# Half of the 64x64 matmuls of the mixers' solve move to the two crossed quadrants of TensorE; GpSimd copies a transposed inverse for them

## The chip, the cores and the metric

The kernel runs on one core of one Trainium2 chip. The metric is the time of one execution on the device, in microseconds (us). The kernel before takes 1534.42 us (median of 3 runs, 1533.93 to 1536.74).

## What is computed

Two small transformer blocks, one after the other, on 256 tokens of width 1024. The change touches only the first block, whose two layers each begin with a mixer; these are called m0 and m1 in the kernel. A mixer has a gated delta rule (in both directions, 4 heads of 128) and an HGRN2 scan beside it. The delta rule needs, for each head, chunk of 64 tokens and direction, the inverse of a unit triangular 64x64 matrix:

```
a = jnp.where(strict, jnp.einsum('bhntd,bhnsd->bhnts', kb, k) * decay, 0.0)
t_inv = lax.linalg.triangular_solve(a + eye, jnp.broadcast_to(eye, a.shape),
                                    left_side=True, lower=True, unit_diagonal=True)
u = jnp.einsum('bhnts,bhnsv->bhntv', t_inv, v * beta[..., None])
w = jnp.einsum('bhnts,bhnsd->bhntd', t_inv, kb * jnp.exp(gc)[..., None])
```

With 4 heads, 4 chunks and 2 directions that is 32 such matrices in a layer. Everything else (projections, convolutions, feed-forward parts, the second block's attention) stays as it is.

## The kernel before

Five engines run their own instruction lists, written out by hand in the order in which they run: TensorE (PE), ScalarE (ACT), VectorE (DVE), GpSimd (POOL) and SyncE for the DMAs. Semaphores join them. An engine that waits for one holds back all that stands behind the wait in its own list. Weights arrive in chunks of 128x2048; ACT rounds a chunk to the high half WH, DVE subtracts to get the low half WL, and PE multiplies with both. Eight PSUM banks are handed out in turn.

The inverses of one direction d (0 or 1) are 16 units of 64x64, eight in the upper 64 partitions and eight in the lower 64, in the buffer XIv; XTv holds their transposes. The solve doubles the inverted blocks level by level (lv 1 to 6). A level is:

- `dn_y(d, lv)` on PE: 16 matmuls of 64x64, those of the upper 64 partitions in one quadrant of the PE array and those of the lower 64 in the opposite one. It waits until the level before has been placed in XIv.
- `dn_y` on ACT: copies the 128x512 product from PSUM to YBv.
- `dn_z(d, lv, 0)` on PE: 16 matmuls of the transposed inverse XTv with YBv. It waits for that copy and for the transposed inverse of the level before.
- `placed(d, lv)` on DVE: a predicated copy of 128x512 from PSUM into XIv under the mask of the level.
- `back(d, lv)` on DVE: transposes XIv into XTv by 32x32 blocks.

The first level is made by `dn_first` on DVE from the matrices themselves. At level 5 PE computes both sides (`dn_z(d, 5, 0)` and `dn_z(d, 5, 1)`) and ACT copies the 32-wide corners of both (`dn_z5`). Level 6 joins the two halves (`dn_y6`, `dn_z6`), and already runs in the two crossed quadrants. `blocks_out` on ACT copies XTv into the full 128x128 form.

Between the steps of the solve stands the work of the HGRN2 part: `z_in(n)` (two subtractions of 128x512 on DVE), `hg_exp(n)` (an exponential of 128x1024 on ACT), `hg_mul(g)` (a product of 128x1024 on DVE), `hg(g)` on PE, and `kept(g)` (a predicated copy on DVE). It goes from DVE to ACT to PE and back: `hg(7)` on PE, the last of them, needs `hg_exp(14)` of ACT, and that needs `z_in(14)` of DVE. PE has pieces of projections between (`zproj`, `gate`), and DVE and ACT prepare the weight chunks (`chunk`).

Of the kernel before, what the change touches and what calls it, by code (L numbers as in the profile page):

```python
# [133 lines left out]
def program(nc, a):  # L134
    P_AT, P_W = par_layout()
    ctx = ExitStack()
    with ctx:
# [151 lines left out]
        HALF = (slice(0, 64), slice(64, 128))  # L289
        att = SB[:, 11264:13312]  # L290
# [42 lines left out]
        def level_mask(kind, lv):  # L333
            return MKv[:, kind, lv, 0:64].unsqueeze(1).to_broadcast([128, 8, 64])
# [80 lines left out]
        def tensor(e):  # L415
# [149 lines left out]
            def mixer(l):  # L565
# [83 lines left out]
                def side_placed(d, lv, side):  # L649
                    w.wait_ge(*(A if lv == 5 else V)["placed", st, d, lv, side])  # L650

                def dn_y(d, lv):
                    w.wait_ge(*V["pair", st, 3, d])
                    side_placed(d, lv - 1, 0)
                    p = bank(st, "y", d, lv)
                    for m in range(8):
                        for h in HALF:
                            last = mm(p[h, m * 64:m * 64 + 64], at_d(d, 1 - m // 4)[h, m % 4, h], XIv[h, d, m], True, True)
                    last.then_inc(*P.up("ps", st, "y", d, lv))
                    ps.give(st, "y", d, lv)  # L660

                def dn_z(d, lv, side):
                    w.wait_ge(*A["y", st, d, lv])
                    side_placed(d, lv - 1, 1)
                    p = bank(st, "z", d, lv, side)
                    for m in range(8):
                        for h in HALF:
                            x, y = XTv[h, d, m], YBv[d][h, m]
                            last = mm(p[h, m * 64:m * 64 + 64], *((x, y) if side == 0 else (y, x)), True, True)
                    last.then_inc(*P.up("ps", st, "z", d, lv, side))  # L670
                    ps.give(st, "z", d, lv, side)

                def dn_y6():
# [3 lines left out]
                    for m in range(8):  # L677
                        for d in range(2):
                            last = mm(p[HALF[1 - d], m * 64:m * 64 + 64], at_d(d, 1 - m // 4)[HALF[d], m % 4, HALF[1 - d]],
                                      XIv[HALF[d], d, m], True, True)  # L680
# [3 lines left out]
                def dn_z6():  # L684
# [4 lines left out]
                    for m in range(8):  # L689
                        for d in range(2):  # L690
                            last = mm(p[HALF[d], m * 64:m * 64 + 64], YBv[0][HALF[1 - d], m], XTv[HALF[1 - d], d, m], True, True)
# [3 lines left out]
                def hg(g):  # L695
# [20 lines left out]
                    ps.give(st, "hg", g, 1)  # L716
# [96 lines left out]
                dn_z(1, 1, 0)  # L813
                dn_z(0, 1, 0)
# [3 lines left out]
                dn_z(1, 2, 0)  # L818
                hg(0)
                dn_y(1, 3)  # L820
                dn_z(0, 2, 0)
                dn_z(1, 3, 0)
# [3 lines left out]
                dn_z(0, 3, 0)  # L826
                dn_z(1, 4, 0)
                dn_y(0, 4)
                hg(1)
                dn_z(0, 4, 0)  # L830
                dn_y(1, 5)
                hg(2)
                dn_z(1, 5, 0)
                dn_z(1, 5, 1)
# [394 lines left out]
        def scalar(e):  # L1229
# [57 lines left out]
            def mixer(l):  # L1287
# [145 lines left out]
                def dn_z5(d, side):  # L1433
                    kind = d if side == 0 else 1 - d
                    w.wait_ge(*P["ps", st, "z", d, 5, side])
                    for b in range(2):
                        cp(corner((XIv, XTv)[side][:, d], b, kind), corner(units(ps[st, "z", d, 5, side][:, :]), b, kind),
                           "placed", st, d, 5, side, of=ps.out(st, "z", d, 5, side))

                def blocks_out(d):  # L1440
                    waits(A["placed", st, d, 5, 1], P["ps", st, "row", 3, 1] if d else P["ps", st, "y6"])
                    for b in range(2):
                        cp(XTF[d][HALF[b], :, HALF[b]], XTv[HALF[b], d], "blocks out", st, d)
# [117 lines left out]
                dn_z5(1, 1)  # L1561
                dn_y(0, 5)
                hg_exp(9)
                hg_exp(8)
                blocks_out(1)
                dn_z5(1, 0)
                dn_z5(0, 0)
# [3 lines left out]
                dn_z5(0, 1)  # L1571
# [407 lines left out]
        def vector(e):  # L1979
# [126 lines left out]
            def mixer(l):  # L2106
# [158 lines left out]
                def dn_first(d):  # L2265
                    waits(A["ident", st], V["pair", st, 3, d])
                    for b in range(2):
                        cpred(XTv[HALF[b], d].rearrange("p (j h) n -> p j h n", j=2),
                              block_mask(b, 1 - d, 0, 4).unsqueeze(1).to_broadcast([64, 2, 4, 64]),
                              AT6[HALF[b], 3 - 2 * d:5 - 2 * d, :, HALF[b]], "placed", st, d, 0, 1)  # L2270
# [124 lines left out]
                z_in(6)  # L2395
                kept(2, after=1)
# [9 lines left out]
                z_in(13)  # L2406
                z_in(12)
# [559 lines left out]
        def gpsimd(e):  # L2967
# [5 lines left out]

            for st in ("m0", "m1"):
                for d in (1, 0):
                    w.wait_ge(*(P["ps", st, "row", 3, 1] if d else P["ps", st, "y6"]))
                    zeros(XTF[d][HALF[1 - d], :, HALF[d]], "zeros", st)
# [159 lines left out]
```

## Time and profile before

| | us |
|---|---|
| median of 3 runs | 1534.42 |
| the profiled execution, its span | 1535.2 |
| PE busy in it | 1508.5 |
| DVE busy | 1200.7 |
| ACT busy | 1015.8 |
| POOL busy | 8.3 |
| solve of m0, from its first matmul on PE to hg(7) | 123.8 to 176.8 |
| solve of m1, from its first matmul on PE | 577.2 |

The profile holds one execution; its span is 0.8 us above the median of the runs. Of an engine it gives when each instruction started and how long it took. Times in it count from the start of the span. A matmul in fp32 shows as two records (two passes), so a step of 16 matmuls is 32 records. A busy PE is not PE at its peak: a pass shows its whole latency, and passes overlap.

### The profile page before, as it was taken

The page shows a single profiled execution, that of the slowest core. Times are in us where ns is not written, and L with a number is a line of the kernel's source. Part 1 is how long each engine was busy: PE and PEld are TensorE (multiplying, and loading weights), DVE is VectorE, ACT ScalarE, POOL GpSimd, SP SyncE. Part 2 cuts the span into 40 slices and gives each one's busy share as a digit, 9 for nine tenths or more (in the row PEclk, how much of TensorE's full clock was granted, in tenths as well). Part 3 has the DMA queues.
Part 4 walks back from the last instruction along what each step waited for, and adds up shares of the span by engine and source line. Part 5 has one row for each costly group of instructions (what it writes and reads, how often), then busy time and mean ns, then how long its engine had stood idle before and what let it go on. Part 6 is the DMA issues. An engine that isn't in the chain of part 4 may idle for free.

```text
span 1535.2 us, 29830 instructions
## 1 busy us (share of the span) xinstructions
PE 1508.5 (98%) x12702; PEld 1403.2 (91%) x12702; DVE 1200.7 (78%) x1693; ACT 1015.8 (66%) x1566; POOL 8.3 (1%) x18
## 2 busy tenths in 40 slices
PE   8999999999999999999999999999999998999998
PEld 8899999988889999999988889968999897899997
DVE  7999766889758799667898768875888578688864
ACT  7786865667646776765776546685777457677753
POOL 0000000000000000000000000000000001000000
PEclk9999999999999999999999999999999999999999
DMA  7522135555554422244655546402655543255551
GB/s 290 192 89 107 56 138 193 200 187 193 207 177 158 158 98 85 84 166 165 236 193 182 212 165 249 155 2 85 218 193 187 193 144 135 83 202 187 190 192 55
DMA packets 35700, 245.55 MB, mean 160 GB/s; under 512 B 4208, under 2 KB 4592, under 8 KB 6512
## 3 DMA queue, kind: packets, MB, share of 16 engines
q1 hardware_dynamic: 35568, 243.65, 44.3%
q8 instruction: 100, 1.64, 0.4%
q14 instruction: 32, 0.26, 0.0%
HBM read 242.58 MB, written 1.05 MB: 159 GB/s over the span
## 4 chain that ended last, share of the span: by engine, by line
PE 84%; DVE 10%; ACT 4%; DMA 1%; issue 1%; SPq 0%; DVEq 0%; ACTq 0%
PE PS L420 83%; DVE WL L1984 2%; DVE SB L1993 1%; DVE SB L1984 1%; DVE SA L1984 1%; ACT WH L1237 1%; ACT SB L1234 1%; DMA RAW<-w_in 1%; PE PS L423 1%; ACT SB L1911 1%; DVE SB L2259 1%; DVE SA L1993 0%; DVE SA L2161 0%; DMA X<-xt 0%; DVE SM L1984 0%
## 5 line engine op out<-in xcount | busy, mean ns | idle before, releaser
L420 PE MATMUL PS<-XHL,WH 128*128 128x256 f32 (+2 forms) x4080 | 846.8, 300 | 6.2 <-DVE WL L1984 3.5
L420 PEld LDWEIGHTS PS<-XHL,WH 128*128 128x128 f32 (+1 forms) x4080 | 644.8, 187 | 43.1 <-issue 5.6
L420 PE MATMUL PS<-XHL,WL 128*128 128x256 f32 (+1 forms) x2392 | 669.5, 280 | 0.0
L1237 ACT CAST WH<-RAW 128x2048 fp32r<-128x2048 f32 (+1 forms) x235 | 427.4, 1822 | 270.8 <-PE PS L420 259.0
L1984 DVE TENSOR_TENSOR WL<-RAW,WH 128x2048 fp32r<-128x2048 f32 (+1 forms) x235 | 511.9, 2181 | 113.2 <-ACT WH L1237 109.4
L420 PEld LDWEIGHTS PS<-XHL,WL 128*128 128x128 f32 (+1 forms) x2392 | 448.3, 187 | 0.4
L420 PE MATMUL PS<-INHL,WH 128*128 128x512 f32 (+1 forms) x1216 | 334.2, 344 | 0.0
L420 PE MATMUL PS<-INHL,WL 128*128 128x256 f32 x960 | 270.0, 281 | 0.0
L420 PEld LDWEIGHTS PS<-INHL,WH 128*128 128x128 f32 x1216 | 210.0, 188 | 27.6
L420 PEld LDWEIGHTS PS<-INHL,WL 128*128 128x128 f32 x960 | 181.2, 189 | 0.0
L1984 DVE TENSOR_TENSOR SB<-SB 128x512 f32<-128x512 f32 (+2 forms) x162 | 108.8, 674 | 14.5 <-ACT SB L1234 11.4
L1237 ACT COPY SB<-PS 128x256 f32<-128x256 f32 (+4 forms) x198 | 84.6, 462 | 42.7 <-PE PS L420 31.5
L1993 DVE SCALAR_TENSOR_TENSOR SB<-SB,PR 128x254 f32<-128x254 f32 (+2 forms) x212 | 95.6, 491 | 15.0 <-ACT SB L1234 11.4
L1234 ACT ACTIVATE SB<-SB,PR 128x256 f32<-128x256 f32 x132 | 78.6, 596 | 17.4 <-DVE SB L1984 17.4
L1234 ACT ACTIVATE SB<-SB 128x512 f32<-128x512 f32 (+3 forms) x103 | 66.0, 643 | 12.4 <-DVE SB L1984 11.1
L420 PE MATMUL PS<-SB 64*64 64x64 f32 (+2 forms) x1680 | 73.1, 227 | 0.6 <-DVE SB L2263 0.6
L420 PEld LDWEIGHTS PS<-SB 64*64 64x64 f32 (+1 forms) x1680 | 66.4, 140 | 3.9 <-DVE SB L2263 0.9
L420 PE MATMUL PS<-SA 128*64 128x64 f32 (+6 forms) x784 | 67.9, 288 | 0.6 <-DVE SA L1984 0.6
L1984 DVE TENSOR_TENSOR SB<-PS,SM 128x512 f32<-128x512 f32 (+2 forms) x65 | 43.9, 677 | 27.6 <-PE PS L420 22.3
L1275 ACT ACTIVATE XHL<-X,PR 128x256 fp32r<-128x256 f32 x56 | 25.1, 501 | 48.3 <-DVE X L1984 23.8
L420 PEld LDWEIGHTS PS<-SA 128*64 128x64 f32 (+3 forms) x784 | 47.2, 157 | 8.7 <-issue 4.1
L1984 DVE TENSOR_TENSOR X<-X,PS 128x256 f32<-128x256 f32 (+1 forms) x72 | 31.7, 449 | 30.0 <-PE PS L420 28.9
(156 smaller groups left out, 1446.0 us busy)
## 6 DMA issues: line engine op xcount, KB each, us to landing
RAW<-w_in SPq DMA_DIRECT2D x51, 1024.0 KB, 4.8
RAW<-w_up SPq DMA_DIRECT2D x44, 1024.0 KB, 4.8
RAW<-f_in SPq DMA_DIRECT2D x44, 1024.0 KB, 4.7
RAW<-w_down SPq DMA_DIRECT2D x22, 1024.0 KB, 4.8
RAW<-f_out SPq DMA_DIRECT2D x22, 1024.0 KB, 4.7
RAW<-a_w_in SPq DMA_DIRECT2D x10, 1024.0 KB, 5.0
RAW<-w_out SPq DMA_DIRECT2D x8, 1024.0 KB, 4.8
RAW<-w_bdn SPq DMA_DIRECT2D x4, 1024.0 KB, 4.8
```

The lines of the kernel that those rows point to most:

```text
L420: return e.matmul(out, l, r, start=start, stop=stop, skip_group_check=True)
L423: return e.transpose(out, x, ident[0:k, 0:k])
L1234: e.activation(out, x, f, bias=bias, scale=scale).then_inc(*A.up(*key, of=of))
L1237: e.copy(out, x).then_inc(*A.up(*key, of=of))
L1275: e.mul(halves_of(st)[0][:, s], X[:, s], norm_gain(st, k)).then_inc(*A.up("x hi", st, k))
L1911: e.activation(pb[:, r * 384 + lo:r * 384 + hi], ps[st, "sc", t_, r][:, lo:hi], ACT.Exp, bias=s[:, i:i + 1], accum_out=s[:, 4 + i:5 + i]). ...
L1984: e.tensor_tensor(out, x, y, op).then_inc(*V.up(*key, of=of))
L1993: e.scalar_tensor_tensor(out=out, in0=x, scalar=s, in1=y, op0=op0, op1=op1).then_inc(*V.up(*key, of=of))
L2259: e.copy_predicated(out, m, data).then_inc(*V.up(*key, of=of))
```

## The change

In every step of levels 1 to 5 half of the units go through the crossed quadrants, so that four quadrants have work. For that the lower half's units are stored turned by four places (`place`). Products whose rows come from the upper partitions go to one PSUM bank and those from the lower to another, so that `dn_y` and `dn_z` take two banks each, and what evacuates them works on two halves of 256 columns. `dn_z` needs XTv of four units in the other 64 partitions: GpSimd copies them (`shifted`, two copies of 64x256 for a direction and level) into the new buffer XTS after `back`. The second side of level 5 is no longer a matmul step: `back5` on DVE transposes the new corners of XIv into XTv, after ACT has copied them (`dn_z5`). The schedules of the engines change where steps fall away or are added; `hg` banks are given back one step later.

```diff
+        XTS = SB[:, 7680:8192].rearrange("p (d m n) -> p d m n", d=2, m=4)
+        YH = [y.rearrange("p (r m n) -> p r m n", r=2, m=4) for y in YBs]
...
+        def place(b, m):
+
+            return (m + 4 * b) % 8
...
                 def dn_y(d, lv):
                     w.wait_ge(*V["pair", st, 3, d])
                     side_placed(d, lv - 1, 0)
-                    p = bank(st, "y", d, lv)
-                    for m in range(8):
-                        for h in HALF:
-                            last = mm(p[h, m * 64:m * 64 + 64], at_d(d, 1 - m // 4)[h, m % 4, h], XIv[h, d, m], True, True)
+                    p = row_banks("y", d, lv)
+                    for m in range(4):
+                        o = slice(m * 64, m * 64 + 64)
+                        for f in range(2):
+                            for b in range(2):
+                                last = mm(p[b][HALF[b ^ f], o], at_d(d, 1 - f)[HALF[b], m, HALF[b]],
+                                          XIv[HALF[b], d, place(b, m + 4 * f)], True, True)
...
-                def dn_z(d, lv, side):
+                def dn_z(d, lv):
                     w.wait_ge(*A["y", st, d, lv])
                     side_placed(d, lv - 1, 1)
-                    p = bank(st, "z", d, lv, side)
...
+                    w.wait_ge(*G["shifted", st, d, lv - 1])
+                    p = row_banks("z", d, lv)
+                    for m in range(4):
+                        o = slice(m * 64, m * 64 + 64)
+                        for f in range(2):
+                            for b in range(2):
+                                r = b ^ f
+                                x = XTS[HALF[r], d, m] if f else XTv[HALF[b], d, place(b, m)]
+                                last = mm(p[r][HALF[b], o], x, YH[d][HALF[r], b, m], True, True)
...
                 hg(2)
-                dn_z(1, 5, 0)
-                dn_z(1, 5, 1)
+                dn_z(1, 5)
                 dn_y(0, 5)
                 zproj(2, 1)
                 hg(3)
-                dn_z(0, 5, 0)
+                dn_z(0, 5)
                 hg(4)
                 dn_y6()
-                dn_z(0, 5, 1)
                 zproj(3, 0)
...
                 def dn_y(d, lv):
                     waits(P["ps", st, "y", d, lv], V["k sum", st, 3] if d == 0 else V["bb", st])
-                    cp(YBv[d], units(ps[st, "y", d, lv][:, :]), "y", st, d, lv, of=ps.out(st, "y", d, lv))
+                    for r in range(2):
+                        cp(YBs[d][:, r * 256:r * 256 + 256], ps[st, "y", d, lv, r][:, 0:256], "y", st, d, lv,
+                           of=ps.out(st, "y", d, lv, r))
...
+                def dn_z5(d):
+                    w.wait_ge(*P["ps", st, "z", d, 5])
+                    for r in range(2):
+                        z = ps[st, "z", d, 5, r][:, 0:256].rearrange("p (m n) -> p m n", m=4)
+                        for b in range(2):
+                            cp(corner(XIv[:, d, 4 * r:4 * r + 4], b, d), corner(z, b, d), "placed", st, d, 5, 0, of=ps.out(st, "z", d, 5, r))
...
                 def placed(d, lv):
-                    w.wait_ge(*P["ps", st, "z", d, lv, 0])
-                    cpred(XIv[:, d], level_mask(d, lv), units(ps[st, "z", d, lv, 0][:, :]), "placed", st, d, lv, 0, of=ps.out(st, "z", d, lv, 0))
+                    w.wait_ge(*P["ps", st, "z", d, lv])
+                    for r in range(2):
+                        z = ps[st, "z", d, lv, r][:, 0:256].rearrange("p (m n) -> p m n", m=4)
+                        cpred(XIv[:, d, 4 * r:4 * r + 4], level_mask(d, lv, 4), z, "placed", st, d, lv, 0, of=ps.out(st, "z", d, lv, r))
+
+                def back5(d):
+                    w.wait_ge(*A["placed", st, d, 5, 0])
+                    for b in range(2):
+                        blocks_turned(corner(XTv[:, d], b, 1 - d), corner(XIv[:, d], b, d), "placed", st, d, 5, 1)
...
+            def shifted(st, d, lv):
+
+                w.wait_ge(*V["k out", st, 3])
+                w.wait_ge(*V["placed", st, d, lv, 1])
+                for b in range(2):
+                    e.tensor_copy(XTS[HALF[1 - b], d], XTv[HALF[b], d, place(b, 4):place(b, 4) + 4]).then_inc(*G.up("shifted", st, d, lv))
...
+                for lv in range(5):
+                    for d in (1, 0):
+                        shifted(st, d, lv)
```

Two places show how the lists move. The first is DVE in m0 after `placed(0, 4)`. SA holds the HGRN2 operands, MK the masks, PS is PSUM. Before, `z_in(6)` (two subtractions) is followed at once by `kept(2)`, `z_in(9)`, `hg_mul(3)`, `z_in(8)` and `hg_mul(4)`:

```order
L1984 TENSOR_TENSOR SA<-SA 128x128x4 x2
L2259 COPY_PREDICATED SB<-MK,PS 128x512 [waits s_dve_done,s_pe_group_done]
L1984 TENSOR_TENSOR SA<-SA 128x64x8 x2
L1984 TENSOR_TENSOR SA<-SA 128x1024 [waits s_act_done]
L1984 TENSOR_TENSOR SA<-SA 128x64x8 x2
L1984 TENSOR_TENSOR SA<-SA 128x1024 [waits s_act_done]
L2263 STREAM_TRANSPOSE SB<-SB 128x512 [waits s_dve_done]
```

And after the change, from the same `z_in(6)` on:

```order
L2007 TENSOR_TENSOR SA<-SA 128x128x4 x2
L2286 STREAM_TRANSPOSE SB<-SB 32x8x32 [waits s_act_done]
L2286 STREAM_TRANSPOSE SB<-SB 32x8x32
L2282 COPY_PREDICATED SB<-MK,PS 128x512 [waits s_dve_done,s_pe_group_done]
L2007 TENSOR_TENSOR SA<-SA 128x64x8 x2
L2007 TENSOR_TENSOR SA<-SA 128x1024
L2007 TENSOR_TENSOR SA<-SA 128x64x8 x2
```

The two transposes of `back5(1)` stand between, and the first of them waits for ACT.

The second place is ACT at the same time. Before: the copies of four `dn_y` steps, `hg_exp(7)` and `hg_exp(6)` (x2), the two corner copies of `dn_z5(1, 1)`, the copy of `dn_y(0, 5)`, `hg_exp(9)` and `hg_exp(8)`:

```order
L1237 COPY SB<-PS 128x512 [waits s_pe_group_done] x4
L1234 ACTIVATE SA<-SA 128x1024 [waits s_dve_done] x2
L1237 COPY SB<-PS 32x8x32 [waits s_pe_group_done]
L1237 COPY SB<-PS 32x8x32
L1237 COPY SB<-PS 128x512 [waits s_pe_group_done]
L1234 ACTIVATE SA<-SA 128x1024 [waits s_dve_done] x2
```

After, from the last `dn_y` copy ahead of the exponentials on:

```order
L1259 COPY SB<-PS 128x256 [waits s_pe_group_done]
L1259 COPY SB<-PS 128x256
L1256 ACTIVATE SA<-SA 128x1024 [waits s_dve_done] x2
L1259 COPY SB<-PS 32x4x32 [waits s_pe_group_done]
L1259 COPY SB<-PS 32x4x32 x3
L1259 COPY SB<-PS 128x256 [waits s_pe_group_done]
L1259 COPY SB<-PS 128x256
L1256 ACTIVATE SA<-SA 128x1024 [waits s_dve_done] x2
```

The corner copies, now of XIv and four of them, still stand behind `hg_exp(6)`, which waits for `z_in(6)` of DVE.

## Rows read from the trace of the kernel before

**Rows 1.** The page: the span, and each engine's busy time.

```profile
span 1535.2 us, 29830 instructions
PE 1508.5 (98%) x12702; PEld 1403.2 (91%) x12702; DVE 1200.7 (78%) x1693; ACT 1015.8 (66%) x1566; POOL 8.3 (1%) x18
```

**Rows 2.** Windows of m0: length; busy us of PE, PEld, DVE, ACT, POOL; clock; DMA.

```profile
114.00:134.60 20.60, 19.77 (x353) 19.14 (x353) 20.47 (x30) 14.48 (x30) 0.00 (x0) 1.00 0.31 114
134.60:156.50 21.90, 21.90 (x536) 21.20 (x537) 20.80 (x30) 12.18 (x17) 0.00 (x0) 1.00 0.27 98
156.50:175.00 18.50, 18.43 (x340) 17.57 (x339) 18.40 (x26) 16.73 (x22) 0.52 (x1) 1.00 0.10 31
182.00:200.00 18.00, 18.00 (x132) 16.91 (x131) 5.97 (x4) 10.63 (x13) 0.00 (x0) 1.00 0.23 71
```

**Rows 3.** The chain that ended last, 108 to 182 us: start, us, what.

```profile
133.39 1.15 DVE SA L1984
...
134.58 37.37 PE PS L420 x846
```

**Rows 4.** Timeline of PE: start, us, instructions [idle before, releaser].

```profile
142.50 5.00 PE L420 MATMUL PS<-SB 64*64 64x64 f32 x160
...
148.51 2.08 PE L420 MATMUL PS<-SB 64*64 64x64 f32 x64
...
160.81 1.91 PE L420 MATMUL PS<-SB 64*64 64x64 f32 x64
...
176.77 1.15 PE L420 MATMUL PS<-SA 128*64 128x64 f32 x32
```

**Rows 5.** Timeline of DVE in m0.

```profile
118.64 0.87 DVE L1993 SCALAR_TENSOR_TENSOR SA<-SA,SM,SB 128x256 f32<-128x256 f32 x2
145.56 0.73 DVE L2259 COPY_PREDICATED SB<-MK,PS 128x512 f32<-128x512 uint8 x1 [0.62 <-PE PS L420]
148.63 1.29 DVE L1984 TENSOR_TENSOR SA<-SA 128x512 f32<-128x512 f32 x2 [0.23 <-PE PS L420]
151.07 1.28 DVE L1984 TENSOR_TENSOR SA<-SA 128x512 f32<-128x512 f32 x2
173.71 1.29 DVE L1984 TENSOR_TENSOR SA<-SA 128x512 f32<-128x512 f32 x2
```

**Rows 6.** DVE groups by shape, 114 to 177 us: busy us, mean ns.

```profile
L1984 DVE TENSOR_TENSOR SA<-SA 128x512 f32<-128x512 f32 x28 | 17.7, 682 | 0.4 <-PE PS L420 0.4
L1984 DVE TENSOR_TENSOR WL<-RAW,WH 128x2048 fp32r<-128x2048 f32 x5 | 11.4, 2272 | 0.0
L1984 DVE TENSOR_TENSOR SA<-SA 128x1024 f32<-128x1024 f32 x8 | 9.7, 1219 | 0.0
```

**Rows 7.** Timeline of ACT in m0.

```profile
152.38 1.06 ACT L1234 ACTIVATE SA<-SA 128x1024 f32<-128x1024 f32 x1 [0.20 <-DVE SA L1984]
153.74 0.75 ACT L1237 COPY SB<-PS 32x256 f32<-32x256 f32 x2 [0.29 <-PE PS L420]
...
175.04 1.06 ACT L1234 ACTIVATE SA<-SA 128x1024 f32<-128x1024 f32 x1 [0.61 <-DVE SA L1984]
```

**Rows 8.** A GpSimd group by shape, whole span: busy us, mean ns.

```profile
L2986 POOL COPY SA<-SB 32x512 f32<-32x512 f32 x4 | 2.8, 694 | 349.9 <-DVE SB L1984 349.7
```

**Rows 9.** Timelines of GpSimd and DVE around 1280 us.

```profile
1280.11 2.95 POOL L2986 COPY SA<-SB 32x512 f32<-32x512 f32 x4 [349.75 <-DVE SB L1984]
...
1281.86 0.72 DVE L1984 TENSOR_TENSOR SM<-SM 128x4 f32<-128x4 f32 x2
1282.50 2.71 DVE L1984 TENSOR_TENSOR WL<-RAW,WH 128x2048 fp32r<-128x2048 f32 x1
```

**Rows 10.** Windows around a fall of PE's clock; columns as in rows 2.

```profile
1291.00:1295.70 4.70, 1.76 (x14) 1.06 (x14) 4.04 (x15) 1.94 (x9) 1.08 (x2) 1.00 0.00 0
1295.70:1299.10 3.40, 3.40 (x19) 2.18 (x17) 1.37 (x7) 3.35 (x16) 0.00 (x0) 0.50 0.00 0
```

More of the change, by code:

```diff
@@ L331, in qk, with level_mask @@
             return QKv[:, d, h, lo:hi]
-        def level_mask(kind, lv):
-            return MKv[:, kind, lv, 0:64].unsqueeze(1).to_broadcast([128, 8, 64])
+        def place(b, m):
+            return (m + 4 * b) % 8
+        def level_mask(kind, lv, n=8):
+            return MKv[:, kind, lv, 0:64].unsqueeze(1).to_broadcast([128, n, 64])
         def block_mask(b, kind, lv, n):
@@ L649, in side_placed, with row_banks, give_rows @@
                 def side_placed(d, lv, side):
-                    w.wait_ge(*(A if lv == 5 else V)["placed", st, d, lv, side])
+                    w.wait_ge(*(A if (lv, side) == (5, 0) else V)["placed", st, d, lv, side])
+                def row_banks(name, d, lv):
+                    return [bank(st, name, d, lv, r) for r in range(2)]
+                def give_rows(name, d, lv):
+                    for r in range(2):
+                        ps.give(st, name, d, lv, r)
                 def dn_y(d, lv):
@@ L812, in mixer @@
                 dn_y(0, 1)
-                dn_z(1, 1, 0)
-                dn_z(0, 1, 0)
+                dn_z(1, 1)
+                dn_z(0, 1)
                 zproj(1, 1)
@@ L817, in mixer @@
                 dn_y(0, 2)
-                dn_z(1, 2, 0)
+                dn_z(1, 2)
                 hg(0)
                 dn_y(1, 3)
-                dn_z(0, 2, 0)
-                dn_z(1, 3, 0)
+                dn_z(0, 2)
+                dn_z(1, 3)
                 zproj(2, 0)
@@ L825, in mixer @@
                 dn_y(1, 4)
-                dn_z(0, 3, 0)
-                dn_z(1, 4, 0)
+                dn_z(0, 3)
+                dn_z(1, 4)
                 dn_y(0, 4)
                 hg(1)
-                dn_z(0, 4, 0)
+                dn_z(0, 4)
                 dn_y(1, 5)
                 hg(2)
-                dn_z(1, 5, 0)
-                dn_z(1, 5, 1)
+                dn_z(1, 5)
                 dn_y(0, 5)
@@ L1431, in dn_y6 @@
                     cp(YBv[0], units(ps[st, "y6"][:, :]), "y6", st, of=ps.out(st, "y6"))
[L1433 to L1438, printed above, removed]
+                def dn_z5(d):
[4 more added lines that the diff above has]
+                            cp(corner(XIv[:, d, 4 * r:4 * r + 4], b, d), corner(z, b, d), "placed", st, d, 5, 0, of=ps.out(st, "z", d, 5, r))
                 def blocks_out(d):
-                    waits(A["placed", st, d, 5, 1], P["ps", st, "row", 3, 1] if d else P["ps", st, "y6"])
-                    for b in range(2):
-                        cp(XTF[d][HALF[b], :, HALF[b]], XTv[HALF[b], d], "blocks out", st, d)
+                    waits(V["placed", st, d, 5, 1], P["ps", st, "row", 3, 1] if d else P["ps", st, "y6"])
+                    cp(XTF[d][HALF[0], :, HALF[0]], XTv[HALF[0], d], "blocks out", st, d)
+                    for f in range(2):
+                        cp(XTF[d][HALF[1], 4 * f:4 * f + 4, HALF[1]], XTv[HALF[1], d, 4 - 4 * f:8 - 4 * f], "blocks out", st, d)
                 def dn_z6(d):
@@ L1560, in mixer @@
                 hg_exp(6)
-                dn_z5(1, 1)
+                dn_z5(1)
                 dn_y(0, 5)
@@ L1570, in mixer @@
                 hg_exp(13)
-                dn_z5(0, 1)
                 hg_exp(12)
@@ L2395, in mixer @@
                 z_in(6)
+                back5(1)
                 kept(2, after=1)
@@ L2406, in mixer @@
                 z_in(13)
+                back5(0)
                 z_in(12)
```

41 lines of the change are left out of this document (22 added, 19 removed).

## The prediction

> **What bounds the kernel now.** The page first: PE is busy 1508.5 of 1535.2 us, POOL 8.3 [rows 1]. That looks as if any work taken from PE were time won. The change sits in one stage of each mixer, so the windows of that stage count. In m0, from 114 to 175 us, PE is busy in 60.1 of 61.0 us, but DVE is busy in 59.7 of them [rows 2]: two engines are full at the same time. Only after 182 us does DVE have room, 5.97 us of 18.0, while PE stays full [rows 2]. The chain that ended last runs through DVE until 134.5 us and then through PE for 37.37 us [rows 3], so PE decides, but by how much is not in the chain; that is the slack of the DVE path, and it is found at the hand-over behind the solve. The last HGRN2 operand is prepared by DVE until 175.00 (173.71 + 1.29) [rows 5], ACT's exponential of it runs from 175.04 to 176.10 [rows 7], and PE starts hg(7), which uses it, at 176.77 [rows 4]. **The slack is 0.67 us.** Over the whole stretch DVE stands idle for hardly more than the gaps of 0.62 and 0.23 us in which it waits for PE [rows 5]. Of what PE is relieved ahead of hg(7), 0.67 us plus those gaps is all that can come out; behind hg(7) the change touches nothing.
>
> **What PE saves.** Five steps in one go, 160 records, take 5.00 us; two steps, 64 records, take 2.08 [rows 4]. Each further step adds (5.00 - 2.08) / 3 = 0.97 us. Whether four quadrants work at once shows where a step in the crossed quadrants (dn_y6) is followed by one in the straight ones (dn_z(0, 5, 1)): those 64 records take 1.91 us instead of 2.08 [rows 4], so where they meet, they overlap. Bounds for the new step are 0.97 (no gain) and 0.49 (half). I take 0.5, since the overlap begins as soon as the list allows. Twenty steps in a mixer save 20 x 0.47 = 9.4 us, the two second sides of level 5 another 1.9: 11.3 us a mixer, 22.6 in all, if PE were the only bound. The Trainium skill, "TensorEngine Tiling (Array Packing)", section Tiling Modes, has four 64x64 tiles work independently. By that the step halves; the trace agrees only at the one meeting.
>
> **What DVE gets to do.** Its list up to z_in(14) is what counts.
> - Eight predicated copies of 128x512 become sixteen of 128x256, and two of the four in dn_first are cut too. From 128x512 to 128x1024 an instruction grows by 1219 - 682 = 537 ns [rows 6]; 256 columns are thus worth 0.27. Two instructions of 128x256 in a row take 0.87 [rows 5], 0.40 apart, so each carries some 0.13 beside its columns. Ten cuts of about 0.1: 1.0 us.
> - back5 is new, four transposes of 256 columns each at 0.27 plus about 0.08: 1.4 us. In return nothing leaves DVE, since PE and ACT had made that side.
> - back5(1) stands right behind z_in(6), which ended at 152.35 (151.07 + 1.28) [rows 5]. It waits for ACT's corner copies, and these stand behind hg_exp(6), which itself waits for z_in(6). So DVE stands still for one exponential, 1.06 us, and four corner copies. Two of 32x256 take 0.75 [rows 7], 0.39 apart; halved in width each costs between 0.19 and 0.39, I take 0.29, so four are 1.2. Together 2.3 us. No cover is possible: DVE's next instructions (kept(2), z_in(9), the products) are queued behind the wait, and through them hg(3) and hg(4) on PE. back5(0) is given more room; its corners should be there when DVE comes to it.
> - GpSimd. A copy of 32x512 takes 0.694 us on average [rows 8]. For 256 columns the bounds are 0.35 and 0.69, I take 0.45; twenty in a mixer are 9.0 us. They don't run beside DVE for nothing: while four such copies ran from 1280.11 to 1283.06, a DVE subtraction of 128x2048 with both inputs in SBUF took 2.71 us [rows 9] where its like take 2.27 [rows 6], and two products of four columns took 0.72 [rows 9]. So a copy stops such a DVE instruction for about its own length. z_in, hg_mul and the weight subtractions are all of that kind. The Trainium skill, "SBUF — State Buffer", section Who interferes with whom, says that the two share a read port that one holds for its whole instruction. By that the cost is zero or whole copies, between 0 and 9.0 us a mixer; the trace agrees with the stop of 0.44 us. Going through the list, in five of the ten cases what stands behind back is a transpose, a read of PSUM or a wait, which hides both copies; in the others one of the two is hidden mostly. Five copies remain: 2.2 us.
> - Against it, the gaps of 0.85 us [rows 5] partly close, since PE comes earlier. Partly: dn_z(1, 4) must now wait for GpSimd's pair behind back(1, 3). I take 0.4.
>
> DVE reaches the end of z_in(14) later by 1.0 + 1.4 + 2.3 + 2.2 - 0.4 = 6.5 us. Less the slack of 0.67, hg(7) starts 5.8 us later. PE alone would not be late: it has 11 us less to do. Its own chain gives about the same time. dn_z(0, 5) waits for back(0, 4) and two copies (0.9), then come hg(4), ACT's corners, dn_y6 and the projections.
>
> ACT gets ten more evacuations (some 0.1 us each); they lie in its waits for PE. DMAs and queues don't move.
>
> **Sum.** m1 has the same lists, so 2 x 5.8 = 11.6 us. The profiled execution of 1535.2 [rows 1] becomes 1546.8. It lies 0.8 above the median of 1534.42, so the forecast for the median is 1546.0.
>
> **Rivals.**
> 1. PE is the bound after all: the engines reorder less tightly than I read, GpSimd costs nothing, and the steps halve. Then 22.6 us go: 1511.8. Against it: DVE's list cannot end earlier than its 59.7 busy us allow, and the slack is 0.67. For anything over 3 us to be won, the DVE list would have to shrink, and it grows. Even with no stall and no GpSimd cost, 2.4 - 0.85 - 0.67 = 0.9 us a mixer are lost. Chance 0.05.
> 2. A mild case: corner copies come early enough, or GpSimd hides behind DVE almost wholly. One of the two costs falls away and gaps close: up to 1.5 us a mixer, at most 1537.4. For it: GpSimd's pair is short. Against it: the wait behind hg_exp(6) is in the lists. Chance 0.10.
> 3. PE's clock falls. With half of its time idle (1.76 busy of 4.70) the clock granted next was 0.50, that is 1.2 GHz, for 3.4 us [rows 10]. In my walk PE stands still for some 3.7 us ahead of hg(3) and 2.8 ahead of dn_z(0, 5), about as idle. What follows, up to 3.4 us at half clock, would lose 1.7, and twice that if the fall lasts longer; PE has no slack there any more. Plus 1.7 to 3.4 us a mixer: 1549.4 to 1552.8. Chance 0.20. The Trainium skill, "TensorE: Matmul & The Clock Gate", section "HAM oscillation — how this bites in real kernels", says that a kernel whose PE waits between short bursts loses the full clock again and again; by that rule this case would be the likelier one, and the row at 1295 agrees.
> 4. Quadrants don't overlap, or the copies of GpSimd block DVE nearly always. Then 10 rather than 6.5 us come to DVE's list: 2 x (10 - 0.67) = 18.7, 1553.1. Chance 0.10.
>
> **How the numbers follow.** The forecast case, slower by 5 to 15 us, gets 0.55. The low end takes in rival 2 in part: with GpSimd at one copy (0.45) and the stall at 1.8 the sum is 2 x (1.0 + 1.4 + 1.8 + 0.45 - 0.85 - 0.67) = 6.3; a little more off for a cheaper back5 gives 1538.5. The high end is rival 4 with a part of rival 3: 1555. What lies outside is rival 1, most of rival 2 and a tail above. A measurement tells 0.2% (3.1 us) from no change. Slower by more than that: the forecast, rivals 3 and 4, and a part of 2: 0.87. Within: 0.08. Faster: 0.05.
>
> **What would show it.** In the changed profile: 32 records of a step in about 0.5 us; an idle gap of about 2.3 us on DVE ahead of the first 32-wide transpose, put down to ACT; weight subtractions above 2.4 us where GpSimd copies; PE idle for some 10 us in the stage, most of it ahead of hg(3) and dn_z(0, 5), and put down to DVE or POOL; hg(7) about 53 + 6 us behind the first step. Wrong would be: a shorter gap on DVE, or GpSimd copies of 0.3 us that block nothing; then the time is near that of before. The forecast falls wholly if DVE's list turns out shorter than 59 us.

## The result and the profile after

| | before | after |
|---|---|---|
| median of the runs, us | 1535.58 (1533.93 to 1537.38, 4 runs) | 1549.71 (1548.06 to 1552.18, 4 runs) |
| profiled execution, span, us | 1535.2 | 1546.3 |
| m0, from the first solve step to hg(7), us | 52.95 | 59.92 |

The ratio of the runs is 1.0095 (95% interval 1.0083 to 1.0107): slower by 14 us, some seven in each mixer. m1 goes the same way: its first step begins at 583.23 and its hg(7) at 642.88, 59.65 us later, where before it was 53.07 (577.25 to 630.32). In the text y(d, lv) and z(d, lv) stand for the PE steps dn_y(d, lv) and dn_z(d, lv). In experiments 2 and 10 one execution each (1842.81 us, the profiled one, and 2119.14 us) fell in the slow state; the medians given there are those of the others, and the stage of experiment 2 is not read from its trace.

The page of the changed kernel, part 1 (busy us, share, instructions), answers to [rows 1]:

```profile
span 1546.3 us, 29682 instructions
PE 1495.9 (97%) x12574; PEld 1388.9 (90%) x12574; DVE 1207.9 (78%) x1721; ACT 1015.4 (66%) x1590; POOL 41.8 (3%) x58
```

PE has 12.6 us less to do and the kernel takes longer. The windows say where, with the columns of [rows 2]: from the first solve step to hg(7), then a stretch behind the stage.

```profile
122.80:182.75 59.95, 47.04 (x1077) 43.96 (x1073) 54.84 (x79) 38.76 (x76) 15.73 (x19) 0.89 0.22 73
...
188.00:206.00 18.00, 18.00 (x132) 16.91 (x131) 5.97 (x4) 10.70 (x13) 0.00 (x0) 1.00 0.21 70
```

The same window of the kernel before:

```profile
123.82:176.77 52.95, 52.23 (x1140) 50.06 (x1136) 51.75 (x67) 39.20 (x64) 0.52 (x1) 1.00 0.24 82
```

Two engines were full; now none is. PE stands idle for 12.9 us, DVE for 5.1, and PE's granted clock averages 0.89 where it was 1.00. Behind the stage nothing differs: 18.00 of 18.00. The loss lies in these 60 us.

PE in m0 (start, busy us; what ended the idle time before in brackets), answers to [rows 4]:

```profile
122.83 0.69 PE L426 MATMUL PS<-SB 64*64 64x64 f32 x32
124.58 1.16 PE L426 MATMUL PS<-SB 64*64 64x64 f32 x64 [1.06 <-DVE SB L2286]
...
133.23 0.69 PE L426 MATMUL PS<-SB 64*64 64x64 f32 x32 [2.40 <-POOL SB L3013]
134.22 3.15 PE L426 MATMUL PS<-SA 128*128 128x128 f32 x16 [0.29 <-DVE SA L2007]
...
159.55 1.97 PE L426 MATMUL PS<-SA 128*64 128x64 f32 x32 [3.43 <-DVE SA L2007]
163.94 1.13 PE L426 MATMUL PS<-SB 64*64 64x64 f32 x32 [2.42 <-POOL SB L3013]
...
171.93 2.22 PE L426 MATMUL PS<-SA 128*64 128x64 f32 x64
...
182.75 1.15 PE L426 MATMUL PS<-SA 128*64 128x64 f32 x32
```

Three things are to be seen. The steps did halve: 64 records in 1.16 us and 32 in 0.69, so a further step adds 0.47 where it added 0.97. PE waits for VectorE and for GpSimd, longest ahead of hg(3) (159.55) and of z(0,5) (163.94), and hg(3) itself, 32 records, then takes 1.97 us where hg(7) takes 1.15. And the granted clock falls twice, not once. The first fall stands behind the wait of 2.40 us at 133.23, and hg(0) (134.22) is slowed by it; the window:

```profile
135.00:138.40 3.40, 3.40 (x52) 3.17 (x54) 2.15 (x5) 1.90 (x1) 0.79 (x2) 0.51 0.58 241
```

DVE, ACT and POOL in m0 (three views), answer to [rows 5, 7]:

```profile
137.40 2.50 DVE L2007 TENSOR_TENSOR SA<-SA 128x512 f32<-128x512 f32 x4 [1.21 <-PE PS L426]
...
141.77 2.25 DVE L2007 TENSOR_TENSOR WL<-RAW,WH 128x2048 fp32r<-128x2048 f32 x1
143.94 1.42 DVE L2007 TENSOR_TENSOR SA<-SA 128x1024 f32<-128x1024 f32 x1
...
155.44 0.90 DVE L2286 STREAM_TRANSPOSE SB<-SB 32x256 f32<-32x256 f32 x2 [2.12 <-ACT SB L1259]
```

```profile
153.35 1.06 ACT L1256 ACTIVATE SA<-SA 128x1024 f32<-128x1024 f32 x1 [1.31 <-DVE SA L2007]
154.32 1.76 ACT L1259 COPY SB<-PS 32x128 f32<-32x128 f32 x6
```

```profile
141.91 2.37 POOL L3013 COPY SB<-SB 64x256 f32<-64x256 f32 x1 [4.80 <-DVE SB L2286]
...
141.91 3.71 POOL L3013 COPY SB<-SB 64x256 f32<-64x256 f32 x2 [4.80 <-DVE SB L2286]
146.04 0.85 POOL L3013 COPY SB<-SB 64x256 f32<-64x256 f32 x2 [0.42 <-DVE SB L2286]
```

The stall ahead of back5(1) is there as forecast, 2.12 us behind one exponential and ACT's corner copies. The GpSimd rows are the new thing. A pair takes 0.85 us at 146.04, where VectorE pauses and then reads PSUM. Beside the weight subtraction the first copy of a pair takes 2.37: it ends at 144.28, just after the subtraction (141.77 + 2.25 = 144.02). The second lasts till 145.62, just after hg_mul (143.94 + 1.42 = 145.36). By these rows a copy that falls beside such an instruction, with both inputs in SBUF, ends only with it, and hg_mul in turn takes 1.42 us where its like took 1.22 [rows 6]. The Trainium skill, "SBUF — State Buffer", section Who interferes with whom, has the shared read port held for a whole instruction; the row agrees. It also shows that the copy is held far longer (2.37 for some 0.43) than VectorE's instruction (1.42 for 1.22), and the z step waits for the copy. What each of the two is worth, experiment 3 measures.

What ends last in the stage is told by the chain (start, us, what):

```profile
161.74 0.64 DVE SB L2286
162.38 0.05 issue
162.43 0.40 POOL SB L3013
162.82 0.06 issue
162.88 0.93 POOL SB L3013
163.81 0.14 issue
163.94 26.07 PE PS L426 x351
```

From z(0,5) at 163.94, which GpSimd's pair released, PE runs to hg(7) and beyond without a wait. ACT's last exponential runs from 181.30 to 182.36, so hg(7) at 182.75 did not wait for DVE's path either, and hg(5) at 171.93 started 0.21 us after its operand was ready (hg_mul(5), 170.50 + 1.22). The two paths end almost together, as in the kernel before, and PE's own ends last. That the prediction had: PE's chain "gives about the same time".

### The profile page after: what moved, and what is told of

Same layout as the page of the kernel before. It is cut to its first block, busy times and chain, and to the rows that moved or that the text cites. A ratio compares the mean times of both kernels' runs of the same rounds, so it can differ in the third digit from the quotient of the medians.

```text
span 1546.3 us, 29682 instructions
## 1 busy us (share of the span) xinstructions
PE 1495.9 (97%) x12574; PEld 1388.9 (90%) x12574; DVE 1207.9 (78%) x1721; ACT 1015.4 (66%) x1590; POOL 41.8 (3%) x58
## 4 chain that ended last, share of the span: by engine, by line
PE 82%; DVE 11%; ACT 4%; issue 1%; POOL 1%; DMA 1%; SPq 0%; DVEq 0%; ACTq 0%
PE PS L426 81%; DVE SA L2007 2%; DVE WL L2007 2%; DVE SB L2282 1%; ACT SB L1256 1%; DVE SB L2007 1%; ACT WH L1259 1%; DVE SB L2016 1%; DVE SB L2286 1%; POOL SB L3013 1%; PE PS L429 1%; ACT SB L1934 1%; DMA RAW<-w_in 1%; ACT SB L1259 1%; DVE SB L2011 0%
## 5 line engine op out<-in xcount | busy, mean ns | idle before, releaser
L426 PE MATMUL PS<-SA 128*64 128x64 f32 (+6 forms) x784 | 71.6, 303 | 7.4 <-DVE SA L2007 7.4
L426 PE MATMUL PS<-SB 64*64 64x64 f32 (+2 forms) x1552 | 56.3, 240 | 17.6 <-POOL SB L3013 12.2
L426 PEld LDWEIGHTS PS<-SB 64*64 64x64 f32 (+1 forms) x1552 | 48.4, 149 | 22.4 <-issue 8.4
L426 PEld LDWEIGHTS PS<-SA 128*64 128x64 f32 (+3 forms) x784 | 50.9, 171 | 15.5 <-ACT SA L1256 7.2
L1256 ACT ACTIVATE SA<-SA 128x1024 f32<-128x1024 f32 (+2 forms) x60 | 45.0, 765 | 22.7 <-DVE SA L2007 22.6
L2007 DVE TENSOR_TENSOR SA<-SA 128x512 f32<-128x512 f32 (+1 forms) x72 | 56.8, 833 | 3.4 <-PE PS L426 3.1
```

The lines of the kernel that those rows point to most:

```text
L426: return e.matmul(out, l, r, start=start, stop=stop, skip_group_check=True)
L1256: e.activation(out, x, f, bias=bias, scale=scale).then_inc(*A.up(*key, of=of))
L2007: e.tensor_tensor(out, x, y, op).then_inc(*V.up(*key, of=of))
```

## The experiments

Medians are compared with 1549.7 us of the changed kernel; the kernel before, run again beside each group, had medians from 1534.6 to 1535.0. The ratio in each case is to the kernel before. Its interval is about 2 us to each side, so a difference between two changed kernels is known to about 3 us: the single costs below are sizes, not exact shares.

### 1. The transposes later (e1_back5_late)

```diff
-                back5(1)
                 kept(2, after=1)
                 z_in(9)
                 hg_mul(3)
+                back5(1)
```

> Only VectorE's list is changed: the pair of transposes back5(1) goes from ahead of kept(2) to behind hg_mul(3), so that ScalarE's copies that it waits for are long done. Theory A (VectorE's list sets the stage, and the 2.12 us for which it stood ahead of back5(1) is real time): hg_mul(3), and with it hg(3), comes about 2.1 us earlier in each mixer, 1549.7 - 4.2 = 1545.5 us (1544.5 to 1546.5). Rival B (the stage is set by GpSimd's copies, by the chain of steps or by TensorE's clock): the wait turns up again ahead of the next instruction, and the time stays within 1 us of 1549.7.

Measured: 1546.44 us (1543.21 to 1548.37), ratio 1.0076 (1.0064 to 1.0089): 3.3 us back, at the upper edge of theory A's range. DVE shows no wait there:

```profile
154.49 2.41 DVE L2007 TENSOR_TENSOR SA<-SA 128x512 f32<-128x512 f32 x3
156.93 0.90 DVE L2286 STREAM_TRANSPOSE SB<-SB 32x256 f32<-32x256 f32 x2
```

On PE the idle time for the most part moved. hg(3) came 3.2 us earlier behind the first step, z(0,5) 2.2, and the wait for GpSimd grew:

```profile
157.04 1.15 PE L426 MATMUL PS<-SA 128*64 128x64 f32 x32 [0.32 <-DVE SA L2007]
162.50 0.69 PE L426 MATMUL PS<-SB 64*64 64x64 f32 x32 [4.30 <-POOL SB L3013]
```

This trace is of the quickest of the five executions (1543.21 us at a mean granted clock of 0.994; the others took 1546.15 to 1548.37 at 0.987 to 0.989). How much of the stall comes back may thus hang on the clock; that was not tested.

### 2. No copies (e2_no_copies)

```diff
-                    w.wait_ge(*G["shifted", st, d, lv - 1])
-                                x = XTS[HALF[r], d, m] if f else XTv[HALF[b], d, place(b, m)]
+                                x = XTv[HALF[r], d, place(r, m)] if f else XTv[HALF[b], d, place(b, m)]
...
-                for lv in range(5):
-                    for d in (1, 0):
-                        shifted(st, d, lv)
```

> GpSimd's twenty pairs of copies are left out, and each z step reads the right operand of its two crossed quadrants from where the inverse already lies (the wrong half, so the values of the solve differ; counts, shapes and quadrants of the matmuls stay). This takes away both what the copies cost VectorE beside them and what z waits for them. Theory A (copies cost mostly the stretch of VectorE's instructions, 1.05 us a mixer by the trace, and its 2.6 us of gaps behind late z steps shrink to about 1.0): 1549.7 - 2 x 2.6 = 1544.5 us (1543 to 1546). Rival B (the waits of 5.8 us a mixer that TensorE has on GpSimd are on the path in full, and the clock stays up as well): 1549.7 - 2 x 5.8 = 1538 us or below. Rival C (the list of VectorE is so full that neither counts): over 1548.5 us.

Measured: 1541.30 us (1540.11 to 1543.30, 4 runs), ratio 1.0044 (1.003 to 1.0058). 8.4 us came back: more than theory A's 5.2, less than B's 11.6. The expectations of experiments 5 and 7 go by a median of 1541.73, and so by 8.0, 3.7 and 4.3 where this text has 8.4, 4.1 and 4.3.

### 3. Copies that nobody waits for (e3_copies_unwaited)

```diff
-                    e.tensor_copy(XTS[HALF[1 - b], d], XTv[HALF[b], d, place(b, 4):place(b, 4) + 4])
+                    e.tensor_copy(XTS[HALF[1 - b], d], cn("I64", 64)[HALF[b]].unsqueeze(1).to_broadcast([64, 4, 64]))
```

with z reading as in experiment 2. GpSimd also waits for each pair before the next. A mixer has ten pairs, that is twenty single copies; the expectation's twenty pairs a mixer are these.

> As the kernel without the copies (z reads the wrong half, the solve's values differ), but GpSimd still issues its twenty pairs a mixer, of the same shape and at the same places in time, from a constant, and nobody waits for them. What is left of their cost is only what they take from the other engines while they run. If they cost VectorE its stretch of 1.05 us a mixer: 2.1 us above the kernel without copies. If GpSimd blocks VectorE as the prediction took it (2.2 us a mixer): 4.4 us above. If the cost of the copies is all in the wait of z: equal to the kernel without copies within 0.5 us.

Measured: 1545.38 us (1544.68 to 1546.25), ratio 1.007 (1.0057 to 1.0084): 4.1 us above experiment 2 and 4.3 under the changed kernel. So the copies' 8.4 us are, within the noise, two halves: what they take from the other engines while they run (the expectation had 2.1 by the lengthened rows or 4.4 by the prediction; the measured 4.1 is nearer the second), and what z waits for them. A pair from a constant is held as long as the real one:

```profile
143.17 3.64 POOL L3012 COPY SB<-C 64x256 f32<-64x256 f32 x2 [5.30 <-DVE SB L2285]
```

### 4. The clock kept up (e4_clock_kept)

```diff
+                def warm(p, n):
+                    for _ in range(n):
+                        mm(p[:, 0:128], ones, ones, True, True)
...
+                    p = row_banks("z", d, lv)
+                    warm(p[0], {(0, 5): 10, (1, 2): 9}.get((d, lv), 0))
                     w.wait_ge(*A["y", st, d, lv])
...
+                    if g == 3:
+                        p = bank(st, "hg", g, 1)
+                        warm(p, 14)
```

> Added to TensorE: 14 matmuls of 128x128 ahead of hg(3)'s waits, 10 ahead of those of z(0,5) and 9 ahead of those of z(1,2), into banks that the following matmuls overwrite, in time in which TensorE only waited (3.43, 2.42 and 2.40 us). Theory A (the clock at 0.5 from 158.84 to 169.08 is on the path): hg(3), z(0,5), hg(4) and y6 take 1.1, 0.7, 1.1 and 1.1 us for 1.97, 1.13, 1.97 and 1.97, and at least half of these 3.0 us comes back in each mixer: 1545 to 1547 us at a granted clock of 0.9 or more there. Rival B (VectorE's list sets the stage, TensorE's speed counts nothing): the clock stays up and the time is within 1 us of 1549.7. If the clock falls all the same, or the added matmuls last longer than the waits, the run tells neither apart.

Measured: 1546.29 us (1544.61 to 1547.41), ratio 1.0075 (1.0062 to 1.0088): 3.4 us back, as theory A had it, from work that is added. No run of the changed kernel here (1548.06 to 1552.18) is as quick. Window of hg(3) to y6, in the changed kernel and in this one (PE's clock is the third number from the end):

```profile
158.00:168.50 10.50, 6.53 (x126) 6.17 (x128) 9.59 (x15) 5.33 (x10) 1.31 (x2) 0.54 0.01 2
```

```profile
158.00:168.00 10.00, 8.68 (x167) 8.02 (x167) 9.91 (x16) 5.58 (x11) 1.31 (x2) 1.00 0.01 2
```

The granted clock was 0.54 and is 1.00, that is 2.4 GHz instead of mostly 1.2. In the changed kernel PE had just been idle for 3.43 us ahead of hg(3). Ahead of z(1,2) the added matmuls keep off the first fall too: hg(0) takes 2.05 us for 3.15. The 3.4 us are for both falls. The Trainium skill, "TensorE: Matmul & The Clock Gate", section "HAM oscillation — how this bites in real kernels", warns that a kernel whose PE keeps waiting between short bursts loses the full clock again and again; these rows agree.

### 5. All three away (e5_all_three_away)

Experiments 1 and 2 together, and added matmuls where this kernel still waits: 9 ahead of hg(0), 10 ahead of z(0,5).

> The three single runs measured 3.3 us for the stall ahead of back5(1), 8.0 us for GpSimd's copies and 3.4 us for the clock, together 14.7 of the 15.1 us that the change cost. Here all three are taken away at once (z reads the wrong half, so the solve's values differ; 9 added matmuls stand ahead of hg(0), 10 ahead of z(0,5)). Theory A (the three are separate costs and nothing else of the change costs anything): 1549.7 - 14.7 = 1535 us, 1534 to 1537; so the halved steps bring nothing even then, because VectorE's list, longer by its cuts and by back5, sets the stage. Rival B (the three overlap: what one gives back the others give back too): 1538 to 1541. Rival C (with them gone the halved steps show, the solve's 12.6 us fewer on TensorE come back in part): below 1533.

Measured: 1537.63 us (1535.75 to 1541.37, 11 runs), ratio 1.0021 (1.0012 to 1.003). 12.1 us came back where the three singly gave 3.3 + 8.4 + 3.4 = 15.1: they are mostly separate but share 3.0 us. That lies between theories A and B. Above all, the kernel is still 2.7 us slower than the one before. The window of its stage, first step to hg(7):

```profile
123.28:177.35 54.07, 47.27 (x1114) 44.15 (x1111) 53.56 (x79) 38.47 (x76) 0.53 (x1) 1.00 0.23 80
```

DVE is busy in 53.56 of 54.07 us, PE in 47.27, the added matmuls included. With these stalls gone it is VectorE's list that the stage lasts. This is the case that the prediction had priced under rival 1, no stall and no GpSimd cost, at 0.9 us a mixer lost; the stage grew by 54.07 - 52.95 = 1.1 us.

### 6. One part alone in the kernel before (e6_back5_alone)

```diff
-                dn_z(1, 5, 1)
...
-                dn_z(0, 5, 1)
...
-                dn_z5(1, 1)
+                dn_z5(1, 0)
...
                 hg_mul(3)
+                back5(1)
...
                 z_in(13)
+                back5(0)
```

> One part of the change alone in the kernel before: the last level's second side is no longer a step on TensorE and two copies on ScalarE but two 32x32 block transposes on VectorE (back5), placed where nothing is waited for (behind hg_mul(3), and behind z_in(13)). The crossed quadrants, the row banks and the copies are not there. TensorE loses 2 x 0.97 x 2 us of steps in each mixer (3.9), VectorE gains 1.8. Theory A (VectorE's list sets the stage after 0.67 us of slack is used): +1.1 a mixer, 1534.6 + 2.3 = 1537 us. Rival B (TensorE set the stage and the two removed steps were on its path): 3 to 7 us faster, 1528 to 1531.5 us. Between them: equal within 1 us.

Measured: 1538.85 us (1537.33 to 1541.46), ratio 1.0025 (1.0014 to 1.0036): 3.9 us slower, with two steps of 0.97 us a mixer gone from PE (1.9, where the expectation wrongly had 3.9 a mixer: that is the sum over both). hg(7) comes at 178.50, 54.76 us after the first step (123.74), where 52.95 had been: 1.8 a mixer, which is just four transposes at 0.45. ACT has less to do in it as well, two copies of 32x256 for each direction. Work moved from PE to DVE costs its full length here. PE waited for it at an earlier hand-over than hg(7), at hg(5):

```profile
167.62 2.29 PE L420 MATMUL PS<-SA 128*64 128x64 f32 x64 [1.89 <-DVE SA L1980]
```

### 7. ScalarE copies (e7_act_copies)

GpSimd's copies are left out, z waits for ScalarE's instead, and each pair stands in ACT's list ahead of a y copy (for (0,4) behind the exponential 9). Two of the ten places are shown.

```diff
+                def shifted(d, lv):
+                    waits(V["k out", st, 3], V["placed", st, d, lv, 1])
+                    for b in range(2):
+                        cp(XTS[HALF[1 - b], d], XTv[HALF[b], d, place(b, 4):place(b, 4) + 4], "shifted", st, d, lv)
...
+                shifted(0, 2)
                 dn_y(0, 3)
+                shifted(1, 3)
                 dn_y(1, 4)
```

> The changed kernel with one edit: the copies of the crossed half go from GpSimd to ScalarE, values as in the changed kernel. Theory A (GpSimd's copies cost VectorE some 3.7 us by what they take from it beside them, measured by the unwaited copies, and 4.3 us by the waits of z; ScalarE's cost VectorE nothing and z only their 0.8 us): 1542 to 1544 us. Rival B (the wait of z is only moved, ScalarE being in turn late): 3.7 us back and no more, 1546, or less than that if the exponentials come late.

Measured: 1549.34 us (1545.88 to 1550.36, 4 runs), ratio 1.009 (1.0077 to 1.0104): nothing gained that can be told, against theory A and worse than B. GpSimd's hold on VectorE is gone, but ACT works its list in order: in the window 122.5 to 184 PE waits 8.3 us for ACT, in seven waits, where it had waited 5.8 for GpSimd and 1.3 for ACT. DVE waits more for PE, and the stall of back5(1) is still there (the trace is of the quickest of the four executions, 1545.88 us):

```profile
145.11 0.77 DVE L2297 COPY_PREDICATED SB<-MK,PS 128x256 f32<-128x256 uint8 x2 [0.74 <-PE PS L426]
150.44 1.29 DVE L2022 TENSOR_TENSOR SA<-SA 128x512 f32<-128x512 f32 x2 [2.35 <-PE PS L426]
156.32 0.90 DVE L2301 STREAM_TRANSPOSE SB<-SB 32x256 f32<-32x256 f32 x2 [2.11 <-ACT SB L1259]
```

### 8 and 9. Complete versions (e9_all_mended, e13_two_mended)

The first is experiment 7 with experiment 1 and 9 and 14 added matmuls ahead of hg(0) and z(0,5); the second keeps GpSimd's copies and takes experiment 1 with 17 added matmuls ahead of z(0,5) and 9 ahead of z(1,2).

> A whole version of the changed kernel: the copies go to ScalarE (each right ahead of its copy of the next y, for (0,4) behind the exponential 9), back5(1) stands behind hg_mul(3), and 9 and 14 added matmuls fill TensorE's waits ahead of hg(0) and z(0,5). Theory A (ScalarE has room in this stage and shares nothing with VectorE; its copies cost only their latency of some 0.8 us a pair against 0.85 to 4.8 on GpSimd): within 2 us of the kernel with all three away, about 1536.5 us, level with the kernel before. Rival B (ScalarE's list, 15 to 20 pieces longer, now makes the exponentials late, and with them VectorE's multiplications): 1540 to 1546. Below 1533 would mean that the halved steps do reach the end.

Measured: 1543.63 us (1543.1 to 1544.49), ratio 1.0059 (1.0045 to 1.0072): rival B's time, 6.0 above the kernel with all three away.

> The changed kernel with its GpSimd copies and its values, and two of the three costs taken away: back5(1) behind hg_mul(3), and added matmuls in TensorE's two longest waits (17 ahead of z(0,5), 9 ahead of z(1,2)). Theory A (stall and clock are separate, as each alone gave 3.3 and 3.4 us): 1549.7 - 6.7 = 1543 us, still 8 us above the kernel before, which is what the copies cost. Rival B (the same time counted twice: the earlier hg(3) only lengthens the wait of z(0,5) for GpSimd): 1545.5 to 1547 us.

Measured: 1543.99 us (1542.49 to 1544.45), ratio 1.0053 (1.0039 to 1.0067): theory A within 1 us. No whole version beats the kernel before.

### 10 to 12. VectorE relieved (e10_before_light, e11_after_light, e12_no_copies_light)

```diff
-                    tt(z, z, hq, ALU.mult, "z mul", st, g)
+                    tt(z[:, 0:64], z[:, 0:64], hq[:, 0:64], ALU.mult, "z mul", st, g)
...
-                    cpred(attc, level_mask(2, HGI[2 * g][1]), units(ps[st, "hg", g, 1][:, :]), "att", st, of=ps.out(st, "hg", g, 1))
+                    cpred(attc[:, :, 0:4], level_mask(2, HGI[2 * g][1])[:, :, 0:4], units(ps[st, "hg", g, 1][:, :])[:, :, 0:4], "att", st, of=ps.out(st, "hg", g, 1))
```

The same edit in the kernel before, in the changed one, and in the changed one with experiments 1 and 2 together. The last has neither the copies nor the place of back5(1) ahead of hg_mul(3).

> The kernel before with VectorE's list made some 12 us a mixer shorter: the eight multiplications hg_mul work on 64 columns for 1024 and the seven masked copies kept on 4 columns of 64 (so the gated part of the scores is not the reference's). It is the measure for the two kernels that follow. TensorE was busy for 54.78 of 55.5 us in this stage [rows 4 show its unbroken run], so both theories expect little: 0.7 us a mixer or less, 1533 to 1535 us.

> The changed kernel with the same work left out of VectorE's list (hg_mul on 64 columns, kept on 4). Theory A (the halved steps are worth up to 11.3 us a mixer on TensorE, and it is VectorE's list alone that hid them; what remains against them are the copies' latency and the clock, 3 to 6 us a mixer): 5 to 16 us under the lightened kernel before, 1518 to 1529 us. Rival B (even with VectorE free, the chain y, copy, z, placed, back, shifted is as long as the stage): within 3 us of it, or slower.

> The lightened changed kernel without GpSimd's copies and with back5(1) behind hg_mul(3) (z reads the wrong half as well). Theory A: nothing but the chain of the steps and TensorE's own work is left, so up to 22 us under the lightened kernel before: 1513 to 1522 us, and at least 4 us under the one with the copies. Rival B (the copies' waits cost nothing once VectorE is free): equal to the one with the copies within 2 us.

Measured: 1531.43 us (10 runs, ratio 0.9983, 0.9974 to 0.9992), 1536.82 (1.0013, 1.0004 to 1.0022) and 1526.83 (0.9947, 0.9935 to 0.9959). The first gained 3.4 us, more than the 0.7 us a mixer expected. The windows from first step to hg(7), in this order, one fence each:

```profile
123.18:174.70 51.52, 51.52 (x1140) 49.80 (x1136) 41.76 (x66) 39.06 (x65) 0.52 (x1) 1.00 0.24 84
```

```profile
123.15:177.90 54.75, 46.28 (x1076) 43.24 (x1072) 44.88 (x79) 39.14 (x77) 12.94 (x19) 0.91 0.23 79
```

```profile
122.45:171.20 48.75, 43.02 (x1076) 40.00 (x1072) 43.43 (x78) 39.32 (x77) 0.52 (x1) 1.00 0.26 89
```

The kernel before becomes bound by PE alone, 51.52 of 51.52 us. VectorE is busy for 41.76 us there instead of 51.75. Against it the changed kernel still loses 5.4 us (rival B), so a full VectorE was not the only thing that hid the halved steps: the copies, the stall of back5(1), still 2.1 us, and the clock (0.91) suffice together. Without the copies and with back5(1) later it is 4.6 us faster than the lightened kernel before and 10.0 faster than the second. Theory A's time (1513 to 1522) was too low, its lead over the second kernel was there. Which part of the 10.0 us the copies have is not told apart from the stall and the clock (1.00 again). Here, and only here, the halved steps reach the end. Even so, 51.52 - 43.02 = 8.5 us less work on PE bring 2.8 us a mixer; for 5.7 us PE waits, 2.8 of them for ACT and 2.6 for DVE.

## Why the prediction held

The forecast was 1546.0 us, the measured time 1549.7, inside its range, and the mechanism in its frame is the one it named: two full engines, work added to VectorE, a stall and GpSimd's copies. How near the number came is in part luck. The costs measured singly (stall 3.3, GpSimd 8.4, back5 3.9, clock 3.4) add to 19.0 us for both mixers, where the forecast's sum was 11.6, with the first three at 4.6, 4.4 and 2.8 and the cuts at 2.0, and gaps of 0.8 and a slack of 1.3 against them. The two largest errors, GpSimd too small and the clock at nothing, were made good by an overlap of the costs that the sum did not have. Point by point:

- **PE decides, DVE is as full.** Right. With all stalls gone DVE fills the stage (experiment 5), and transposes moved to it cost their length (experiment 6).
- **Steps halve.** Right: 0.47 us for 0.97. Of the 11.3 us a mixer that this was to take from PE, 8.5 show as less busy time at full clock (51.52 - 43.02, experiments 10 and 12); the rest was not looked for.
- **Slack 0.67 us.** Too large: it was read at the last hand-over, hg(7), and an earlier one was tighter. In the kernel before, hg_mul(5) ended at 164.22 + 1.22 = 165.44 and hg(5), which uses it, started at 165.66, 0.22 later:

```profile
164.22 1.22 DVE L1984 TENSOR_TENSOR SA<-SA 128x1024 f32<-128x1024 f32 x1
...
165.66 2.21 PE L420 MATMUL PS<-SA 128*64 128x64 f32 x64
```

  In experiment 6, where PE waited for it, hg(5) came 0.15 us after it (166.25 + 1.22 = 167.47, then 167.62). That leaves 0.07 us of slack, and hg(7) fell 1.8 us behind for 1.8 us of transposes.
- **Cuts, 1.0 us a mixer.** Too much. Two pieces of 128x256 take 0.77 to 0.78 us in a row where one of 128x512 took 0.73 [rows 5]: about 0.05 each, 0.5 in all. Experiments 5 and 6 differ by only 1.2 us, the wrong way for a cost of cuts: beside the gaps that closed it can't be seen. The cuts were not run by themselves.
- **back5, 1.4 us.** It took 1.8: a transpose of 32x256 lasts 0.45, not 0.35. Experiment 6 measured 3.9 us for both mixers.
- **The stall, 2.3 us.** 2.12 in the trace. Taking it away brought 3.3 us for both mixers rather than 4.2, as z(0,5) still waited for GpSimd.
- **GpSimd, 2.2 us.** The term of the sum that was most off. Its cost beside VectorE was near (4.1 us in both mixers for 4.4). What the prediction lacked is the other side: the copy is itself held, up to 2.37 us for one of about 0.43. The prediction's own row, a subtraction of 2.71 us for 2.27, showed VectorE's side alone. The hold made z late, and the prediction counted these waits for next to nothing, 0.9 us for a pair and 0.45 us a mixer that the gaps close less. They are worth 4.3 us. All in all 8.4 for 4.4.
- **Rival 3, the clock.** It came true on top of the forecast case: 0.50 for most of hg(3) to y6, and 0.51 behind the wait ahead of z(1,2), which the prediction did not have. Priced at 1.7 to 3.4 us a mixer, it measured 1.7 for both falls. (The row behind it, 1.76 us busy of 4.70, is 37%, so more than the half idle that the rival says.) It had a chance of 0.20 as an alternative; it was an addition that the forecast's own idle times brought about, and should have stood in the sum.
- **Rival 1**, PE as the bound after all, fell: no kernel with the full VectorE list came under the kernel before. **Rival 2** fell: both waits were there. **Rival 4** had the overlap of the quadrants wrong. That the copies weigh more than the sum had was right, but by z's waits and not by blocking VectorE nearly always.

The four single costs add to 19.0 us and the change cost 14.1 to 15.1, so they overlap. Which microsecond belongs to which was not settled further. In experiment 7 the loss to ScalarE's order is read from the trace and was not tested by itself. What the copies' waits cost through PE's clock was not separated from the waits either: experiment 2 takes the copies, their waits and what follows from them away at once.

## What to carry to other kernels

Where two engines are full in the same stage, look at every hand-over between them, not only the last, before work is taken from one: here halving the steps of one brought nothing, and each microsecond given to the other cost a microsecond. Count a helper copy on GpSimd not by its own length but by the longest VectorE instruction with both inputs in SBUF that it can fall beside (2.37 us for 0.43 here), and ask who waits for it. TensorE may pay for idle time a second time in clock; matmuls that do nothing, placed in the wait, gave 3.4 us back here, and are a cheap test for it.

## What was not expected of the hardware

- GpSimd copies of 64x256 from SBUF lasted from 0.43 us (half of a pair of 0.85) to 2.37 us, according to the VectorE instruction beside them. Copies from a constant tensor behaved the same (3.64 for a pair). VectorE's 128x1024 product beside them grew from 1.22 to 1.42.
- TensorE's granted clock went to 0.54 on average between 158.00 and 168.50 us, behind a wait of 3.43 us, and to 0.51 between 135.00 and 138.40, behind one of 2.40; with added matmuls in these waits and in the one ahead of z(0,5) it stayed at 1.00, and the kernel with more work was 3.4 us faster.
- A 64x64 step whose records use all four quadrants adds 0.47 us for 0.97, with no loss from the crossed ones.
